# Second mixer of a fused three-layer kernel: the gated recurrence's work re-ordered on four engines' queues

## The chip, the core and the metric

One core of a Trainium2 chip runs the whole program. The time is that of the device, in microseconds (us), from three runs of the kernel before; a separate profiled execution gives the trace.

## The reference, cut to what matters

The program is two blocks in a row on 512 tokens of width 1024. The first block (two layers, each a mixer and a convolution FFN) is not touched. The second block's mixer is touched. It projects the normed input to 26 feature tiles of 128 (attention queries, keys, values; `hq`, `i`, `ff`, `fb`, `hg` for the recurrence), and the normed context of 256 tokens for 14 of them:

```python
def hgrn2_prep(q, i, f, lb_d):
    fg = lb_d + (1.0 - lb_d) * jax.nn.sigmoid(f)
    qh = sh(jax.nn.silu(q) * (HG_HEAD_DIM ** -0.5))
    return qh, sh(1.0 - fg), sh(i), sh(jnp.log(fg))
# S_t = diag(f_t) S_{t-1} + k_t v_t^T, o_t = S_t^T q_t, forward and backward, 4 heads,
# the state of the context is where the tokens start; then
# rmsnorm(o_f + flip(o_b), gain) * silu(g), beside softmax attention over 768 keys,
# both into @ w_out, and a SwiGLU FFN
```

## The kernel before, in words

Arrays lie with features on the 128 partitions and tokens on the free axis. A projection's weights come in chunks of 128x1024 (one output tile). For each chunk SP loads 512 KB, ACT makes the high part `w_hi` (line 160), DVE the low part `w_lo` (166), and PE runs three matmuls for each of 8 pieces of the depth (196).

**The slots.** In the mixer PE's work for chunks 2 to 25 is cut into 76 slots (`PARTS`). A chunk with a context half has four slots (two of 12 matmuls on 512 tokens, which I call x slots, then two of 12 on 256 context tokens, c slots). The others have two x slots. `SB_LIST` gives the order of the chunks, `FIRST` a chunk's first slot, `ENDED` the slot at which a chunk has ended. Each engine's program is written out by hand over these slots. What it does in slot p comes in a fixed order, and every engine executes its own queue in that order.

**The recurrence.** There are 4 heads, two directions each (u = 0 to 7), and 7 levels for each direction: 56 jobs, n = 7u + level. One job goes through DVE `difference` (2278, 2279), ACT exponential (`decays`, 2145), POOL's two products into `gla_mixed` (2043, 2044), PE `level` (2432, 8 matmuls) and DVE `select` (2301). The rings are short: `dec` has 4 buffers, so a difference waits for the product of job n - 4. `gla_mixed` has 3, so the product of job n waits for `level` n - 3. `level` waits for `select` n - 2.

**Around the jobs** lies work of each head or direction, placed with `due(n, first, every, number)`:
- ACT `sigmoid` of the gates (2081); from head 2 on it is preceded by the query's Silu (2076). POOL `gates` (2009), keys (2014, 2015) and their sum (2019). ACT `gate_logs` (2087), which waits for the keys. DVE `sum_gates` (four scans, 2265, 2267). All this has to be done for a head before its first difference.
- ACT `prepare` (2096 to 2100); POOL `to_end` (2024, 2025); PE `turn_values` and `turn_keys` (2442, 2449), all through PSUM bank 5; ACT `v_out` (2117) and `kd_out` (2109), which empty that bank one turn at a time; PE `sums` (2459, 2462); DVE `states`.
- PE `diagonal`, `output` and `mean`; ACT `diag_out`, `o_out` (2130, 2131) and `o_rstd` (2137 a logarithm, 2139 an exponential); DVE's scaling with it (2318).

Before, DVE, ACT and POOL are at job p - 11 in slot p (`AHEAD`) and PE at job p - 14 (`PE_AT`). `result(c)` on ACT empties a chunk's banks (2066 for the context, which bank 2 holds alone, 2069 for the tokens) and then makes `w_hi` of chunk c + 2. The first c slot of a chunk waits for the context copy of the chunk before. At slot 72 ACT runs `head_rstd` (2177, 2180), the attention's six rstd tiles. After the last slot come the splits of keys and queries (2221, 2202), the Silu of the four `hg` tiles (2225) and 32 units of attention (`logits` 2563, 2564; softmax 2238, 2385, 2390; transposes; values 2591).

ACT has function tables: where one instruction needs another set than the one before, the program holds an ACT_TABLE_LOAD. Silu, Sigmoid, Ln and Exp each have one of their own in the trace.

Of the kernel before, what the change touches and what calls it, by code (L numbers as in the profile page):

```python
# [78 lines left out]
def build(nc, A, out):  # L79
    with ExitStack() as ctx:  # L80
# [1682 lines left out]
        def layer(l, out_name, x_base=None, mods=None):  # L1763
# [18 lines left out]
        SB_LIST = [("hq", 0), ("hq", 1), ("ff", 0), ("fb", 0), ("i", 0), ("ff", 1), ("fb", 1), ("i", 1),  # L1782
                   ("hq", 2), ("ff", 2), ("fb", 2), ("i", 2), ("hq", 3), ("ff", 3), ("fb", 3), ("i", 3),
# [83 lines left out]
        ctx_out, hg_in, late_hi = sem("ctx_out"), sem("gate_in"), sem("late_hi")  # L1867
# [11 lines left out]
        AHEAD = 11  # L1879
        PE_AT = 14  # L1880
# [89 lines left out]
        class SecondMixer(Stage):  # L1970
# [26 lines left out]
            def gpsimd(self, pool):  # L1997
# [6 lines left out]
                def gates(hd):  # L2004
                    pool.wait_ge(g["sig"], 4 * hd + 5)
                    for d in range(2):
                        u, t = 2 * hd + d, d * HG + hd
                        for f in (bx(u), bc(u)):
                            nc.gpsimd.tensor_scalar(f, f, lbs[:, 5, t:t + 1], lbs[:, 0, t:t + 1], ALU.mult, ALU.add)\
                                .then_inc(g["fg"], 1)  # L2010
                    for d in range(2):
                        u = 2 * hd + d
                        pool.wait_ge(g["fg"], 2 * u + 2)
                        nc.gpsimd.tensor_scalar(kx[:, u % 4, :], bx(u), -1.0, 1.0, ALU.mult, ALU.add).then_inc(g["k"], 1)
                        nc.gpsimd.tensor_scalar(kc[u % 4][:, :], bc(u), -1.0, 1.0, ALU.mult, ALU.add).then_inc(g["k"], 1)
                    pool.wait_ge(g["k"], 4 * hd + 4)
# [18 lines left out]
                gates(0)  # L2035
                for n in range(JOBS):
# [19 lines left out]
            def scalar(self, act):  # L2056
# [5 lines left out]
                def result(c):  # L2062
# [4 lines left out]
                    if name == "hg":  # L2067
                        act.wait_ge(g["mult"], JOBS)
                    self.emptied(nc.scalar.activation(sb_hT[:, X_TILE[name](m), :], bank[c % 2][:, :],
                                                      ACT.Silu if c < SPLIT else ACT.Copy), c)  # L2070
                    self.high(act, 0, c, c + SPLIT < w.n)

                def sigmoid(hd):
                    if hd >= 2:
                        self.there(act, SB_LIST.index(("hq", hd)))
                        nc.scalar.activation(hq(hd), hq(hd), ACT.Silu)
# [64 lines left out]
                def decays(n):  # L2141
# [4 lines left out]
                    hd = due(n, 2, 2 * LEVELS, HG)  # L2146
# [36 lines left out]
                for p in range(len(PARTS)):  # L2183
                    if p in ENDED:
                        result(ENDED[p])
                    hd = due(p, 20, 14, HG - 1)
                    if p == 8 or hd is not None:
                        sigmoid(0 if p == 8 else hd + 1)
                    hd = due(p, 23, 14, HG - 1)
                    if p == 11 or hd is not None:  # L2190
                        gate_logs(0 if p == 11 else hd + 1)
                    decays(p - AHEAD)
# [4 lines left out]
                    if p == 72:  # L2197
                        head_rstd()
# [19 lines left out]
                act.wait_ge(b["scaled"], NT)  # L2218
                for kv in range(2):
# [3 lines left out]
                for m in range(HG):  # L2223
                    self.there(act, SB_LIST.index(("hg", m)))
                nc.scalar.activation(sb_hT[:, HG_TILE:HG_TILE + HG, :], sb_hT[:, HG_TILE:HG_TILE + HG, :], ACT.Silu).then_inc(hg_in, 1)
                for u in range(U2 + HIGH + 1):
                    if u < TAIL:
                        decays(len(PARTS) - AHEAD + u)
# [21 lines left out]
            def vector(self, dve):  # L2250
# [9 lines left out]
                def sum_gates(hd):  # L2260
                    dve.wait_ge(g["ln"], 4 * hd + 4)
                    dve.wait_ge(g["inside"], 2)
                    for u in (2 * hd, 2 * hd + 1):
                        turn = slice(None, None, 1 if u % 2 == 0 else -1)
                        nc.vector.tensor_tensor_scan(bx(u)[:, turn], inside[:, :], bx(u)[:, turn], 0.0, ALU.mult, ALU.add)\
                            .then_inc(g["scan"], 1)
                        nc.vector.tensor_tensor_scan(bc(u)[:, turn], bc(u)[:, turn], bc(u)[:, turn], 0.0, ALU.add, ALU.bypass)\
                            .then_inc(g["scan"], 1)
# [35 lines left out]
                def gla(n):  # L2304
                    hd = due(n, -1, 2 * LEVELS, HG)
# [4 lines left out]
                    u = due(n, 10, LEVELS, U7)  # L2310
# [4 lines left out]
                    hd = due(n, 26, 2 * LEVELS, HG)  # L2315
                    if hd is not None:
# [449 lines left out]
```

## Time and profile before

| what | us |
|---|---|
| three runs, lowest, median, highest | 2270.62, 2271.0, 2272.22 |
| the profiled execution | 2270.88 |
| its span | 2269.2 |
| PE busy | 2097.4 (92%) |
| DVE, ACT, POOL busy | 1239.7, 902.1, 317.0 |
| mean granted clock of PE | 0.962 |
| first recurrence level on PE, last | 1406.0, 1683.7 |

Times within the span count from its start. A busy share says how long an engine had an instruction running. A stall is time in which PE had none. The granted clock says at which of its two levels (1.2 and 2.4 GHz) PE ran: 1.00 is 2.4 GHz all the time.

### The profile page before, as it was taken

To read this page: it belongs to the slowest core of one execution; us is meant where nothing else is said; L and a number is where in the kernel's file an instruction comes from. 1 tells how busy PE (TensorE), PEld (TensorE's weight loads), DVE (VectorE), ACT (ScalarE), POOL (GpSimd) and SP (SyncE) were. 2 spreads that over 40 slices of the span, in tenths; PEclk is the share of its full clock that TensorE was granted. 3 is DMA by queue.
4 is the path that set the end of the run, shared out by engine and by line. 5 is a ranking of instruction groups with operands and counts; after the bars stand their busy time and mean duration, and the time that the engine had idled before them with its cause. 6 is when DMAs were issued, how large, how long until landed. Compare 5 with 4: busy or idle time off the path is not lost. (4 is left out here: it accounts for less than half of the span.)

```text
span 2269.2 us, 27321 instructions
## 1 busy us (share of the span) xinstructions
PE 2097.4 (92%) x9710; PEld 1660.5 (73%) x9710; DVE 1239.7 (55%) x1922; ACT 902.1 (40%) x1396; POOL 317.0 (14%) x404
## 2 busy tenths in 40 slices
PE   8999878999999899999999978878887898999997
PEld 6666547888888777778888847767765676888886
DVE  3666437788767656756564353555556534333333
ACT  4433533444422344344442244455447624223222
POOL 0033310101000211000000023455420002000000
PEclk9999899999999999999999989889898999999999
DMA  5211002556444322222333212100110022232321
GB/s 182 77 55 38 1 19 75 172 189 194 156 160 156 102 84 84 75 84 92 94 107 106 91 37 65 38 29 29 56 47 1 1 75 66 92 102 92 118 92 50
DMA packets 52628, 191.84 MB, mean 85 GB/s; under 512 B 5792, under 2 KB 8512, under 8 KB 52288
## 3 DMA queue, kind: packets, MB, share of 16 engines
q1 hardware_dynamic: 44672, 163.07, 22.3%
q0 software_dynamic: 7344, 27.27, 3.8%
q8 instruction: 50, 0.82, 0.1%
q10 hardware_dynamic: 528, 0.40, 0.1%
q14 instruction: 34, 0.28, 0.0%
HBM read 187.05 MB, written 3.67 MB: 84 GB/s over the span
## 5 line engine op out<-in xcount | busy, mean ns | idle before, releaser
L196 PE MATMUL psum<-xH,w_hi 128*128 128x512 f32 x1800 | 731.0, 406 | 42.8 <-DVE xL L1301 22.7
L196 PE MATMUL psum<-xL,w_hi 128*128 128x512 f32 x1800 | 713.1, 396 | 0.0
L196 PE MATMUL psum<-xH,w_lo 128*128 128x512 f32 x1800 | 712.7, 396 | 0.0
L166 DVE TENSOR_TENSOR w_lo<-w_raw,w_hi 128x1024 fp32r<-128x1024 f32 (+1 forms) x273 | 355.5, 1303 | 381.4 <-ACT w_hi L160 381.3
L160 ACT ACTIVATE w_hi<-w_raw 128x1024 fp32r<-128x1024 f32 (+1 forms) x273 | 303.1, 1111 | 399.7 <-PE psum L196 395.2
L196 PEld LDWEIGHTS psum<-xH,w_hi 128*128 128x128 f32 x1800 | 345.1, 192 | 144.2 <-DVE xL L1301 37.9
L196 PEld LDWEIGHTS psum<-xH,w_lo 128*128 128x128 f32 x1800 | 345.0, 192 | 74.5
L196 PEld LDWEIGHTS psum<-xL,w_hi 128*128 128x128 f32 x1800 | 345.5, 192 | 71.2 <-issue 3.1
L196 PE MATMUL psum<-hidH,w_hi 128*128 128x512 f32 x528 | 206.2, 391 | 0.0
L196 PE MATMUL psum<-hidH,w_lo 128*128 128x512 f32 x528 | 205.4, 389 | 0.0
L196 PE MATMUL psum<-hidL,w_hi 128*128 128x512 f32 x528 | 205.4, 389 | 0.0
L1376 DVE SCALAR_TENSOR_TENSOR gate_value<-psum,cols,gate_value 128x511 f32<-128x511 f32 x88 | 66.0, 750 | 132.2 <-ACT gate_value L1349 131.2
L1349 ACT ACTIVATE gate_value<-psum,cols 128x512 f32<-128x512 f32 x88 | 60.7, 689 | 162.6 <-PE psum L196 162.6
L1312 POOL TENSOR_SCALAR xT<-y,cols 128x512 f32<-128x512 f32 x32 | 39.4, 1240 | 555.6 <-DVE y L1293 555.6
L196 PEld LDWEIGHTS psum<-hidH,w_hi 128*128 128x128 f32 x528 | 99.1, 188 | 21.0 <-issue 0.5
L196 PEld LDWEIGHTS psum<-hidL,w_hi 128*128 128x128 f32 x528 | 99.1, 188 | 20.9 <-issue 0.5
L196 PEld LDWEIGHTS psum<-hidH,w_lo 128*128 128x128 f32 x528 | 99.1, 188 | 20.7
L2301 DVE COPY_PREDICATED gla_weights<-gla_masks,psum 128x512 f32<-128x512 uint8 x56 | 41.3, 738 | 76.9 <-PE psum L2432 75.2
L2145 ACT ACTIVATE sb_hT<-sb_hT 128x512 f32<-128x512 f32 x56 | 34.9, 629 | 112.4 <-DVE sb_hT L2279 112.3
L612 ACT ACTIVATE logits<-logits,stat 128x128 f32<-128x128 f32 (+3 forms) x64 | 36.0, 562 | 108.2 <-DVE stat L740 108.0
L740 DVE CUSTOM_DVE_ANT_0 logits<-psum,addend 128x128 f32<-128x128 f32 (+3 forms) x64 | 31.4, 490 | 83.7 <-PE psum L846 81.7
L2432 PE MATMUL psum<-gla_mixed 128*128 128x128 f32 x448 | 62.3, 284 | 13.8 <-POOL gla_mixed L2044 13.8
(314 smaller groups left out, 2546.4 us busy)
## 6 DMA issues: line engine op xcount, KB each, us to landing
w_raw<-in_up SPq DMA_DIRECT2D x132, 512.0 KB, 3.5
w_raw<-in_down SPq DMA_DIRECT2D x48, 704.0 KB, 4.0
mod_raw<-in_mod POOLq DMA_DIRECT2D x48, 512.0 KB, 3.9
w_raw<-in_sb_in SPq DMA_DIRECT2D x26, 512.0 KB, 3.5
w_raw<-in_ev_in SPq DMA_DIRECT2D x23, 512.0 KB, 3.6
w_raw<-in_od_in SPq DMA_DIRECT2D x20, 512.0 KB, 3.5
w_raw<-in_ev_out SPq DMA_DIRECT2D x8, 512.0 KB, 3.6
w_raw<-in_od_out SPq DMA_DIRECT2D x8, 512.0 KB, 3.5
```

Source lines behind the costliest of these rows:

```text
L160: nc.scalar.activation(w_hi[:, s % SPLIT, 0:w.cols], raw[:, s, 0:w.cols], ACT.Copy).then_inc(w.high, 1)
L166: nc.vector.tensor_tensor(w_lo[:, s % SPLIT, 0:w.cols], raw[:, s, 0:w.cols], w_hi[:, s % SPLIT, 0:w.cols].bitcast(F32), ALU.subtract).then ...
L196: mm = nc.tensor.matmul(acc, a[:, slot % SPLIT, cut], b[:, k0 + k, :], start=start and n == 0, stop=stop and n == 2)
L612: nc.scalar.activation(t, t, ACT.Exp, bias=stat[:, 0, s:s + 1], scale=-1.0, accum_out=stat[:, 1, s:s + 1]).then_inc(a["exp"], 1)
L740: nc.vector.tensor_tensor_reduce(out=tl[:, s % RING, 0:n], in0=logits_bank(s)[:, 0:n], in1=Xa[:, s % 3, 0:n], scale=-1.0 if kind == "a" el ...
L1312: nc.gpsimd.tensor_scalar(dst, yt[:, t % 3, 0:self.n], self.gain(t), self.shift(t), ALU.mult, ALU.add)\
L1349: nc.scalar.activation(value if j % 2 else gate, bank[j % 2][:, :], ACT.Copy, scale=self.tap(i, j, 2)).then_inc(ff["tap"], 1)
L1376: nc.vector.scalar_tensor_tensor(y[:, 1:T], acc[:, 0:T - 1], self.tap(i, j, 1), y[:, 1:T], ALU.mult, ALU.add).then_inc(ff["conv"], 1)
L2145: nc.scalar.activation(d, d, ACT.Exp).then_inc(g["exp"], 1)
L2301: nc.vector.copy_predicated(aT[:, hd % 2, :, :], level_mask[d][:, l * P:(l + 1) * P].unsqueeze(1).to_broadcast([P, NB, P]), bank[3 + n % 2 ...
L2432: mm = nc.tensor.matmul(bank[3 + n % 2][:, blk(c)], x[:, blk(c)], x[:, blk(c)], start=True, stop=True)
```

## The change

It touches the second mixer alone. The output, the matmuls and the loads stay the same. Chunks `hq2` and `hq3` come forward to places 4 and 5 of the order. ACT, DVE and POOL are at job p - 14 in slot p and PE at job p - 19. What was done per head in one go is spread over more slots.

```diff
-        SB_LIST = [("hq", 0), ("hq", 1), ("ff", 0), ("fb", 0), ("i", 0), ("ff", 1), ("fb", 1), ("i", 1),
-                   ("hq", 2), ("ff", 2), ("fb", 2), ("i", 2), ("hq", 3), ("ff", 3), ("fb", 3), ("i", 3),
+        SB_LIST = [("hq", 0), ("hq", 1), ("ff", 0), ("fb", 0), ("hq", 2), ("hq", 3), ("i", 0), ("ff", 1), ("fb", 1), ("i", 1),
+                   ("ff", 2), ("fb", 2), ("i", 2), ("ff", 3), ("fb", 3), ("i", 3),
...
-        AHEAD = 11
-        PE_AT = 14
+        AHEAD = 14
+        LEAD = LAG = 5
+        PE_AT = AHEAD + LEAD
+        SIGMOID = {8: 0, 24: 1, 36: 2, 48: 3}
+        LOGS = {11: 0, 27: 1, 39: 2, 53: 3}
...
+                gates_at = {c - AHEAD: hd for c, hd in SIGMOID.items() if hd}
...
-                    if l == 2:
+                    if l == 5:
                         to_end(u)
-                    hd = due(n, 9, 2 * LEVELS, HG - 1)
-                    if hd is not None:
-                        gates(hd + 1)
+                    for d in range(2):
+                        if n - d in gates_at:
+                            gates(gates_at[n - d], d)
+                    if n - 2 in gates_at:
+                        keys(gates_at[n - 2])
+                    if n - 3 in gates_at:
+                        key_sum(gates_at[n - 3])
...
-                        act.wait_ge(g["mult"], JOBS)
+                        act.wait_ge(g["mult"], JOBS - 4 + m + 1)
...
-                                                      ACT.Silu if c < SPLIT else ACT.Copy), c)
+                                                      ACT.Silu if name in ("hq", "hg") else ACT.Copy), c)
...
-                    if hd:
-                        act.wait_ge(g["y"], hd)
+                    act.wait_ge(*((g["y"], hd) if hd else (g["to_end"], 4)))
...
+                def around(n):
+                    hd = due(n, LEAD - 1, 2 * LEVELS, HG)
                     if hd is not None:
                         diag_out(hd)
-                    u = due(n, 1, LEVELS, U7)
+                    u = due(n, 4, LEVELS, U7)
                     if u is not None:
                         prepare(u)
                     for half in range(2):
-                        hd = due(n, 4 + half, 2 * LEVELS, HG)
+                        hd = due(n, LEAD + 2 * half, 2 * LEVELS, HG)
                         if hd is not None:
                             v_out(hd, half)
-                        u = due(n, 6 + half, LEVELS, U7)
+                        u = due(n, LEAD + 4 + 2 * half, LEVELS, U7)
                         if u is not None:
                             kd_out(u, half)
-                    hd = due(n, 22, 2 * LEVELS, HG)
+                    hd = due(n, LEAD + 18, 2 * LEVELS, HG)
                     if hd is not None:
                         o_out(hd)
-                    hd = due(n, 24, 2 * LEVELS, HG)
-                    if hd is not None:
+                    hd = due(n, LEAD + 20, 2 * LEVELS, HG)
+                    if hd not in (None, 2):
                         o_rstd(hd)
...
                 for p in range(len(PARTS)):
+                    decay(p - AHEAD)
                     if p in ENDED:
                         result(ENDED[p])
...
+                    if p in SIGMOID:
+                        sigmoid(SIGMOID[p])
+                    if p in LOGS:
+                        gate_logs(LOGS[p])
+                    around(p - AHEAD)
...
                     if p == 72:
+                        o_rstd(2)
                         head_rstd()
...
                 act.wait_ge(b["scaled"], NT)
+                act.wait_ge(g["kv"], U7)
...
-                for m in range(HG):
-                    self.there(act, SB_LIST.index(("hg", m)))
-                nc.scalar.activation(sb_hT[:, HG_TILE:HG_TILE + HG, :], sb_hT[:, HG_TILE:HG_TILE + HG, :], ACT.Silu).then_inc(hg_in, 1)
...
+                def jobs(n):
+                    hd = due(n, 0, 2 * LEVELS, HG)
                     if hd is not None:
-                        sum_gates(hd)
+                        sum_gates(2 * hd)
                     if 0 <= n < JOBS:
                         difference(n)
...
+                def around(n):
+                    hd = due(n, 3, 2 * LEVELS, HG)
+                    if hd is not None:
+                        sum_gates(2 * hd + 1)
+                    u = due(n, LEAD + 8, LEVELS, U7)
                     if u is not None:
                         states(u)
-                    if 3 <= n < JOBS + 3:
-                        select(n - 3)
...
+                    if LAG <= n < JOBS + LAG:
+                        select(n - LAG)
...
+                dve.wait_ge(g["kv"], U7)
+                for n in range(2):
+                    dve.wait_ge(b["v_turned"], n + 1)
...
                 def gla(n):
                     if 0 <= n < JOBS:
                         level(n)
...
+                    for half in range(2):
+                        hd = due(n, 2 * half - 1, 2 * LEVELS, HG)
+                        if hd is not None:
+                            turn_values(hd, half)
+                        u = due(n, 3 + 2 * half, LEVELS, U7)
+                        if u is not None:
+                            turn_keys(u, half)
+                    u = due(n, 7, LEVELS, U7)
+                    if u is not None:
+                        sums(u)
-                    hd = due(n, 18, 2 * LEVELS, HG)
+                    hd = due(n, 17, 2 * LEVELS, HG)
                     if hd is not None:
                         output(hd)
```

`sum_gates` takes one direction instead of a head, DVE's `jobs` comes before the low part of a chunk, and `o_rstd` of head 3 and its scaling now fall into units 5 and 7 of the attention.

## Rows read from the trace of the kernel before

**Rows 1.** The page: PE's busy time, share of the span, instructions.
```profile
PE 2097.4 (92%) x9710; PEld 1660.5 (73%) x9710; DVE 1239.7 (55%) x1922; ACT 902.1 (40%) x1396; POOL 317.0 (14%) x404
```
**Rows 2.** Busy time by stretch: PE, PEld, DVE, ACT, POOL, PE's granted clock, DMA.
```profile
1375.00:1693.70 318.70, 262.53 (x1577) 227.95 (x1575) 168.38 (x262) 152.24 (x262) 142.79 (x169) 0.92 0.12 37
1400.00:1421.00 21.00, 14.49 (x80) 12.27 (x80) 12.54 (x20) 10.73 (x21) 9.31 (x12) 0.84 0.16 49
1581.40:1606.00 24.60, 13.25 (x58) 10.96 (x57) 9.27 (x15) 9.03 (x15) 13.28 (x19) 0.65 0.08 22
1646.70:1693.70 47.00, 39.10 (x191) 29.79 (x189) 24.28 (x36) 15.81 (x26) 14.74 (x13) 1.00 0.08 23
```
**Rows 3.** Waits of PE between 1375 and 1840: us, times, longest.
```profile
PE psum L2449 <- ACT gla_kd_tm L2109: 23.8, 5, 7.2
```
**Rows 4.** Timeline of PE, levels of head 0: start, length (us).
```profile
1426.65 1.06 PE L2432 MATMUL psum<-gla_mixed 128*128 128x128 f32 x8
1428.98 1.06 PE L2432 MATMUL psum<-gla_mixed 128*128 128x128 f32 x8
1433.74 1.05 PE L2432 MATMUL psum<-gla_mixed 128*128 128x128 f32 x8
1437.37 1.05 PE L2432 MATMUL psum<-gla_mixed 128*128 128x128 f32 x8
```
**Rows 5.** Timeline of POOL, ACT and DVE, change from head 2 to head 3.
```profile
1576.89 0.74 POOL L2043 TENSOR_TENSOR gla_mixed<-sb_hT 128x256 f32<-128x256 f32 x1 [7.93 <-ACT sb_hT L2145]
...
1578.47 1.20 POOL L2024 TENSOR_TENSOR gla_keys_decayed<-gla_keys_decayed,gla_k 128x384 f32<-128x384 f32 x1
...
1580.35 1.20 POOL L2009 TENSOR_SCALAR sb_hT<-sb_hT,gla_lb 128x512 f32<-128x512 f32 x1
...
1583.90 0.62 POOL L2014 TENSOR_SCALAR gla_k<-sb_hT 128x512 f32<-128x512 f32 x1
...
1585.88 0.63 ACT L2087 ACTIVATE sb_hT<-sb_hT 128x512 f32<-128x512 f32 x1 [2.78 <-POOL gla_kc L2015]
...
1587.66 1.28 ACT L2145 ACT_TABLE_LOAD   x1
...
1591.32 1.28 DVE L166 TENSOR_TENSOR w_lo<-w_raw,w_hi 128x1024 fp32r<-128x1024 f32 x1 [8.57 <-ACT w_hi L160]
1592.52 1.21 DVE L2265 TENSOR_TENSOR_SCAN sb_hT<-gla_inside,sb_hT 128x512 f32<-128x512 f32 x1
...
1595.94 0.39 DVE L2278 TENSOR_TENSOR sb_hT<-sb_hT 128x256 f32<-128x256 f32 x1
...
1596.70 0.63 ACT L2145 ACTIVATE sb_hT<-sb_hT 128x512 f32<-128x512 f32 x1 [5.41 <-DVE sb_hT L2279]
```
**Rows 6.** Timeline of ACT at 1496.5: `prepare`, `o_out`, `result`, then a table load.
```profile
1496.53 0.62 ACT L2096 ACTIVATE gla_since<-sb_hT 128x512 f32<-128x512 f32 x1
...
1498.33 0.57 ACT L2130 ACTIVATE sb_hc<-psum 128x512 f32<-128x512 f32 x1
...
1499.28 0.37 ACT L2066 ACTIVATE sb_hc<-psum 128x256 f32<-128x256 f32 x1
...
1501.11 1.28 ACT L2076 ACT_TABLE_LOAD   x1
1502.40 0.63 ACT L2076 ACTIVATE sb_hT<-sb_hT 128x512 f32<-128x512 f32 x1
```
**Rows 7.** Timeline of ACT, end of the slots.
```profile
1695.00 1.28 ACT L2177 ACT_TABLE_LOAD   x1
...
1704.11 0.57 ACT L2069 ACTIVATE sb_hT<-psum 128x512 f32<-128x512 f32 x1
...
1710.13 1.70 ACT L2221 ACTIVATE keys_split<-keys 64x768 fp32r<-64x768 f32 x2
```
**Rows 8.** Timeline of PE, logits of unit 0 and of unit 7.
```profile
1713.68 0.55 PE L2563 MATMUL psum<-keys_split,queries_split 128*128 128x256 f32 x1 [3.21 <-DVE queries_split L2367]
...
1735.13 0.36 PE L2563 MATMUL psum<-keys_split,queries_split 128*128 128x256 f32 x1
```

More of the change, by code:

```diff
@@ L2002, in gpsimd, with gates, keys @@
                 pool.wait_ge(g["lb"], LB_STEPS)
-                def gates(hd):
+                def gates(hd, d):
                     pool.wait_ge(g["sig"], 4 * hd + 5)
[L2006 to L2010, printed above, removed]
+                    u, t = 2 * hd + d, d * HG + hd
+                    for f in (bx(u), bc(u)):
+                        nc.gpsimd.tensor_scalar(f, f, lbs[:, 5, t:t + 1], lbs[:, 0, t:t + 1], ALU.mult, ALU.add)\
+                            .then_inc(g["fg"], 1)
+                def keys(hd):
                     for d in range(2):
@@ L2033, in rotated @@
                         .then_inc(b["cos"], 1)
-                gates(0)
+                gates(0, 0)
+                gates(0, 1)
+                keys(0)
+                key_sum(0)
+                gates_at = {c - AHEAD: hd for c, hd in SIGMOID.items() if hd}
                 for n in range(JOBS):
@@ L2067, in result @@
                     if name == "hg":
-                        act.wait_ge(g["mult"], JOBS)
+                        act.wait_ge(g["mult"], JOBS - 4 + m + 1)
                     self.emptied(nc.scalar.activation(sb_hT[:, X_TILE[name](m), :], bank[c % 2][:, :],
-                                                      ACT.Silu if c < SPLIT else ACT.Copy), c)
+                                                      ACT.Silu if name in ("hq", "hg") else ACT.Copy), c)
                     self.high(act, 0, c, c + SPLIT < w.n)
                 def sigmoid(hd):
-                    if hd >= 2:
-                        self.there(act, SB_LIST.index(("hq", hd)))
-                        nc.scalar.activation(hq(hd), hq(hd), ACT.Silu)
+                    self.there(act, SB_LIST.index(("hq", hd)))
                     self.there(act, SB_LIST.index(("ff", hd)))
@@ L2222, in scalar @@
                     queries_high(0, kv)
[L2223 to L2225 removed]
                 for u in range(U2 + HIGH + 1):
                     if u < TAIL:
[L2228 removed]
+                        around(len(PARTS) - AHEAD + u)
                     if OUT <= u < U2 + OUT:
@@ L2258, in gain_of, with sum_gates @@
                     return cols[:, at_g:at_g + 1]
-                def sum_gates(hd):
-                    dve.wait_ge(g["ln"], 4 * hd + 4)
+                def sum_gates(u):
+                    dve.wait_ge(g["ln"], 2 * u + 2)
                     dve.wait_ge(g["inside"], 2)
[L2263 to L2268, printed above, removed]
+                    turn = slice(None, None, 1 if u % 2 == 0 else -1)
+                    nc.vector.tensor_tensor_scan(bx(u)[:, turn], inside[:, :], bx(u)[:, turn], 0.0, ALU.mult, ALU.add)\
+                        .then_inc(g["scan"], 1)
+                    nc.vector.tensor_tensor_scan(bc(u)[:, turn], bc(u)[:, turn], bc(u)[:, turn], 0.0, ALU.add, ALU.bypass)\
+                        .then_inc(g["scan"], 1)
                 def difference(n):
@@ L2338, in vector @@
                         self.low(dve, 0, 0, True)
+                    jobs(p - AHEAD)
                     if p in ENDED and ENDED[p] + SPLIT < w.n:
@@ L2343, in vector @@
                         nc.vector.tensor_copy(level_mask[p - 2][:, :], masks_in[p - 2][:, :])
-                    gla(p - AHEAD)
+                    around(p - AHEAD)
+                    if p == 73:
+                        normed(2)
                     if p in GAINS:
@@ L2378, in vector @@
                     if u < TAIL:
-                        gla(len(PARTS) - AHEAD + u)
+                        around(len(PARTS) - AHEAD + u)
                     if 0 <= v < U2:
@@ L2395, in vector @@
                     if hd is not None:
-                        dve.wait_ge(hg_in, 1)
+                        self.there(dve, SB_LIST.index(("hg", hd)))
                         dve.wait_ge(g["y"], hd + 1)
@@ L2493, in gla @@
                         level(n)
-                        u, l = n // LEVELS, n % LEVELS
-                        if l < 2 and u % 2 == 0:
-                            turn_values(u // 2, l)
-                        if l in (2, 3):
-                            turn_keys(u, l - 2)
-                        if l == 5:
-                            sums(u)
-                    hd = due(n, 18, 2 * LEVELS, HG)
+                    for half in range(2):
[9 more added lines that the diff above has]
+                    hd = due(n, 17, 2 * LEVELS, HG)
                     if hd is not None:
                         output(hd)
-                    hd = due(n, 20, 2 * LEVELS, HG)
+                    hd = due(n, 19, 2 * LEVELS, HG)
                     if hd is not None:
@@ L2552, in logits @@
                     else:
[L2553 removed]
+                        pe.wait_ge(b["v_out"], 1)
                         pe.wait_ge(g["pred"], JOBS)
```

47 lines of the change are left out of this document (18 added, 29 removed).

## The prediction

> **What bounds the kernel now.** I read the page first. PE is busy 92% of the span [rows 1], so only work taken off PE, or stalls and slow clock taken away, can shorten the run. This change takes nothing off PE. So I asked how much PE stands still in the second mixer. Up to 1693.7, where slot 72 begins, the busy time by stretch gives 318.7 - 262.5 = 56.2 us of stall, and a granted clock of 0.92: 2 x 0.08 x 318.7 = 51 us at 1.2 GHz instead of 2.4 [rows 2]. Some 28 of these 51 are stall (the three long waits below and a little before each). In the other 23 the work took twice its time, so the clock cost 11.7. Together 67.9 us stand to be had before slot 72. They lie in four places. The start, 1400 to 1421: 21.0 - 14.5 = 6.5 of stall, clock 0.84 [rows 2]. Three changes of head, alike: 24.6 - 13.25 = 11.35 in the one shown, clock 0.65 [rows 2]. Slots 62 to 71: 47.0 - 39.1 = 7.9 [rows 2]. Short waits between: the rest, 56.2 - 6.5 - 34.0 - 7.9 = 7.8. The waits say what ends a change of head: five waits of PE for `kd_out`, 23.8 us, the longest 7.2 [rows 3]. The timeline of the other engines shows the chain behind it: POOL's product, `to_end`, gates, keys, then ACT's logarithms (ACT had waited 2.78 for them), ACT's high part, DVE's low part, four scans, difference, exponential [rows 5]. ACT and DVE take their queues in order, so copies that PE needs stand behind this chain.
>
> **Durations.** From one level to the next PE takes 2.33 in a c slot and 3.63 in an x slot; a level is 1.05, or 0.85 of PE's time in sequence [rows 4]. The product of a job takes 1.58 (1576.89 to 1578.47), `to_end` 1.88, gates 3.55, keys 1.98, four logarithms 1.78, the low part 1.20, two scans 1.71 (half of 1592.52 to 1595.94), a difference 0.76 [rows 5]. `prepare` takes 1.80, `o_out` 0.95, `result` with a context copy 1.83, a table load 1.28 with 0.63 for the function behind it [rows 6]. Other copies on ACT are taken at 0.4 to 0.6, as those.
>
> **Part by part.** *The start.* Job 0's product was late for PE's slot 14. Now ACT, DVE and POOL begin it three slots later and PE five. The three chunks ahead of it have two slots less of context, and the Silu of `hq2` and `hq3` adds two loads (2.6) to ACT, which waits for PE at each chunk anyway. Gone through queue by queue with the durations above, an estimate: the first product is there near 1409, and PE comes to it near 1416. The cover is 7 us; I cost the start at 0 (was 6.5 and some 2.1 of clock).
>
> *The change to head 1.* The gates' pieces hang on jobs 10 to 13, and `mixed` has three buffers: the product of job 12 waits for level 9, in PE's slot 28. ACT's logarithms stand in slot 27, so ACT stands still until PE is past slot 28. From the start of level 9: 1.2 to the product, 1.6 product, 1.9 `to_end`, 2.0 keys, 0.9 two logarithms, 1.7 scans, 0.8 difference, 0.6 exponential, 0.4 context copy: 11.1. PE needs that copy for slot 30, at 5.0. Next late is DVE's low part, and behind it the select for level 11: 14.4 against 6.4. Cost 8.0, and 1.2 of clock.
>
> *To head 2.* Keys again wait, for level 21 in slot 40. ACT in slot 39 has the logarithms, `prepare(3)` and `kd_out(2, 1)`, which PE's `sums(2)` needs right after level 21. Chain: 1.2 + 1.6 + 2.0 + 1.8 + 1.3 (load for the exponential) + 1.8 + 0.4 = 10.1, against 0.9. The grouping with `o_rstd(0)` gives nothing, since `prepare(3)` stands between: two more loads and 1.3 us of functions, one exponential, `result` 1.8, low part 1.2, select 0.7, and level 23 comes at 18.2 against 7.1. Cost 11.1, clock 0.6 (its own wait covers the rest).
>
> *To head 3.* Sigmoid stands 8 slots ahead. Only `sums(4)` in slot 54 waits, 10.1 against 7.3: 2.8, and 1.0 of clock. The three changes: 9.2 + 11.7 + 3.8 = 24.7, where they cost 34.0 and 9.6.
>
> *New short waits.* `to_end(u)` now comes after level 5's product, which waits for PE's slot 7u + 21, and `turn_keys` wants it in slot 7u + 22: 4.7 after that level's start against 3.2 where a c slot lies between (slots 22, 43, 50: 1.5 each) and 4.5 elsewhere (0.2): 5.3 in all. `turn_values` of heads 1 to 3 (slots 32, 46, 60) wants `kd_out` of ACT's same slot, behind `prepare` and `diag_out`: 3.1, 1.4 and 3.1, by the same addition. In slots 62 to 71 the attention's means wait for DVE's select and rotation as before: 0.6 + 1.4 + 1.0 + 2.1 = 5.1 (was 7.9, of which the moved `o_rstd(2)` was 2.1). The last is larger than before, as Silu's load now stands in `result(22)`, ahead of DVE's low part. Sum before slot 72: 24.7 + 5.3 + 7.6 + 5.1 = 42.7, against 67.9.
>
> *From slot 72 on.* Three levels, a sum and a transpose move behind the mark: -4.4 before it. ACT empties chunk 23 and, 0.1 before the mark, starts `o_rstd(2)` (3.9) and `head_rstd` (1704.11 - 1695.00 = 9.1 [rows 7]), then a load, Silu and `kd_out(7, 1)`: +15.2. PE, ready at +14.5, does `sums(7)` to 16.6. Now both engines wait for it, DVE copies values and scales (4.3), and the splits begin at +20.9; they began at 1710.13, +16.4 [rows 7]. First logits 3.55 later [rows 7, 8], at +24.5; they were at +20.0. Then I save the Silu of `hg` (1.9 and a load) and `o_rstd(3)` in front of the second exponential, and pay `states(7)`, `output(3)` at half clock, `mean(3)` and `o_rstd(3)` (3.8) in units 0 to 5. Worked through unit by unit, unit 7's logits come at +48.3; they were at +41.4 (1735.13 [rows 8]). +6.9, of which 4.4 is the moved work. Beyond unit 7 nothing differs. The weights' loads keep their number; two go four to eight places earlier on SP's queue, which has had the buffers free each time, and no wait is added on it.
>
> **Sum.** 42.7 - 67.9 - 4.4 + 6.9 = -22.7. The profiled execution took 2270.9 (span 2269.2, 1.7 around it) and stands 0.1 under the median 2271.0: 2248.2, and 2248.3 against the median. I say 2248.
>
> What the trace does not show is how low the clock falls after the new stalls. From below it costs nothing after them; from above all work for 6 us after each of three, as in the stretch at 0.65 [rows 2], 3 x 3 = 9. I took 2.8, nearer the low end, since new waits cover part of it.
>
> **Rivals.** *A, the leads cover the changes of head.* If POOL runs so far ahead that keys and logarithms are done before ACT is wanted, the three changes cost nothing: 2248 - 25 = 2223. For it speaks the distance of 5 jobs; against it the ring of three, which pins POOL to three jobs ahead of PE. *B, the waits only move.* The chain behind a level is as long as before, so each change costs what it did, 14.5 with its clock: 43.6 instead of 24.7, giving 2267, within 0.2% of no change (a measurement of this kernel can tell about that much). For it: POOL still follows PE, and 11 us of chain is no shorter. Against it: at head 3 five slots lie between. *C, slower: both chains at each change.* If the copy for the context (8.0) and `kd_out` (11.1) are late one after the other at all three, with 3 of clock, each costs 22: 66 instead of 24.7, giving 2290. It decides once a change costs over 17 on average. Against it: by the slots the two are late together only at head 2.
>
> *D, the tables.* If a change of table held ACT 1.4 longer than the load, as long again, head 2 would cost 4 more and the end, with its five changes, 7 more: 2248 + 11 = 2259. If a logarithm and an exponential needed only one load between them, the grouping would be idle and the end 5 shorter: 2243. Against both: the function starts 0.01 behind its load [rows 6], and `head_rstd` begins with a load for its logarithms [rows 7] though exponentials ran before it. Both lie inside the forecast's own range, chance together 0.01, counted with it.
> The Trainium skill (ScalarE: Activation LUTs, What ACT_TABLE_LOAD costs) states the first: 1283 ns of load and some 1380 ns of drain for each switch; this trace shows the load and no drain.
> The same page (Table sets) states the second, one load for a logarithm followed by an exponential; this trace doesn't agree.
>
> That the order isn't what it says can't be, as each queue is written out.
>
> **Chances.** Forecast 0.70, A 0.12, B 0.09, C 0.09. Faster by over 0.2% (4.5 us): forecast and A, 0.82. Same: B, 0.09. Slower: C, 0.09. The forecast's own range: the small waits and clock together can be off by some 18 either way, 2230 to 2267. Reaching to B's side makes it 2230 to 2268. It leaves out A and C, 0.21.
>
> **What would show it.** Right: no stall between slots 12 and 22; waits of PE for a context copy near 6 us at slot 30, for `kd_out(2, 1)` near 9 at slot 40, under 4 at slot 54; many waits for `to_end` of about 1.5; ACT waiting for the keys at two changes; a load between the logarithms of slot 39 and `o_rstd(0)`; a gap of some 8 us before the first logits. Wrong: no wait of PE over 3 us at slots 28 to 42 (A); a stall of 11 at head 3 too (B, C); a first logit earlier than 23 after slot 72, or units 5 to 7 with no gap.

## The result, and the profile after

| | median us | runs | ratio to the kernel before, 95% interval |
|---|---|---|---|
| before | 2271.6 | 4 | |
| after | 2286.2 | 4 | 1.0064 [1.0049, 1.0079] |

The change is 14.6 us slower; the forecast was 2248, 23 us faster, with a range to 2268. Of the four places in which the prediction saw 67.9 us to be had, the start gave its share and the changes of head gave a part. Slots 62 to 71, which it had left nearly alone, took more than that back.

The page gives the busy time of each engine. PE does the same number of instructions as in [rows 1]:

```profile
PE 2100.3 (92%) x9710; PEld 1664.0 (73%) x9710; DVE 1240.8 (54%) x1922; ACT 899.8 (39%) x1394; POOL 321.5 (14%) x404
```

Busy time by stretch, with the columns of [rows 2]: the mixer up to slot 72, its start, the changes to head 1 and to head 2, and slots 61 to 71:

```profile
1375.00:1700.40 325.40, 263.88 (x1529) 229.23 (x1528) 162.05 (x250) 148.15 (x256) 143.24 (x166) 0.92 0.12 36
1404.50:1425.50 21.00, 21.00 (x137) 19.03 (x137) 15.04 (x26) 11.29 (x22) 10.03 (x12) 1.00 0.21 71
1446.00:1480.20 34.20, 22.76 (x124) 20.04 (x123) 17.07 (x24) 13.76 (x26) 17.04 (x21) 0.84 0.10 31
1500.00:1555.00 55.00, 37.40 (x226) 33.60 (x225) 28.80 (x42) 24.38 (x43) 26.10 (x31) 0.84 0.06 20
1618.90:1700.40 81.50, 63.11 (x300) 49.12 (x299) 31.17 (x53) 24.59 (x43) 24.14 (x28) 0.90 0.08 26
```

Slot 72 begins at 1700.4, where it began at 1693.7. The start is full, 21.00 busy of 21.00, at a granted clock of 1.00. Slot 61 begins at 1619.0, before the change at 1633.3: 14.3 us had been won by there. Slots 61 to 71 then take 81.5 us where they took 60.4 (1633.3 to 1693.7), with 18.4 us of stall and a clock of 0.90.

The waits of PE up to slot 72 (line waited on, releaser; total, times, longest), where [rows 3] had five long ones for `kd_out`:

```profile
PE psum L2480 <- ACT gla_kd_tm L2121: 14.4, 3, 8.8
PE psum L2463 <- ACT gla_kd_tm L2121: 12.5, 3, 5.4
PE psum L2549 <- ACT sb_hT L2185: 8.1, 2, 7.6
PE psum L196 <- ACT sb_hc L2080: 7.5, 1, 7.5
PE psum L2470 <- POOL gla_keys_decayed L2031: 5.9, 5, 1.9
PE psum L2549 <- ACT gla_k L2185: 5.5, 1, 5.5
PE psum L2544 <- DVE head_sin L2348: 4.8, 3, 2.0
...
```

With the two groups below them (2.2 and 0.5) they add up to 61.5 us (56.2 before). L2480 is `sums` and L2463 `turn_values`. L2549 is `head_turn`, PE's turn of an attention tile for its rotary embedding, and L2544 the mean of such a tile. L196 with L2080 is the context copy, L2470 `turn_keys`. The two waits of 7.6 and 5.5 at `head_turn` were in no step of the prediction. The timelines of POOL, DVE, ACT and PE around the first of them (start, length, instruction; in brackets the idle time ahead of it and what ended it) show where it is from:

```profile
1659.71 0.73 POOL L2053 TENSOR_TENSOR gla_mixed<-sb_hT 128x256 f32<-128x256 f32 x1 [5.92 <-PE psum L2453]
...
1661.08 1.26 POOL L2038 TENSOR_TENSOR head_rot<-sb_hT,rope 128x512 f32<-128x512 f32 x1
1653.99 0.68 DVE L2348 TENSOR_TENSOR head_sin<-psum,rope 128x512 f32<-128x512 f32 x1
1662.45 0.69 DVE L2352 TENSOR_TENSOR sb_hT<-head_rot,head_sin 128x512 f32<-128x512 f32 x1 [7.77 <-POOL head_rot L2038]
1663.85 0.63 ACT L2156 ACTIVATE sb_hT<-sb_hT 128x512 f32<-128x512 f32 x1 [12.06 <-DVE sb_hT L2289]
...
1666.44 0.58 ACT L2185 ACTIVATE sb_hT<-psum 128x512 f32<-128x512 f32 x1
1658.51 1.05 PE L2453 MATMUL psum<-gla_mixed 128*128 128x128 f32 x8
1667.16 2.05 PE L2549 MATMUL psum<-sb_hT,rope_turn 128*128 128x512 f32 x2 [7.60 <-ACT sb_hT L2185]
```

A tile's rotation has two halves: POOL multiplies by the cosines (`rotated`, L2038), DVE by the sines (L2348), and DVE adds them (L2352). POOL's half for turn v stands behind job n = c - 13, c being the slot in which DVE scales that tile (`GAINS`). The line reads `n + AHEAD - 1 in GAINS` in both kernels, but `AHEAD` went from 11 to 14: before, it was job c - 10. With three buffers job n's product waits for level n - 3. PE now does that level in slot n + 16 = c + 3; before, it did it in slot n + 11 = c + 1. DVE wants the rotation in slot c + 2 (c + 3 for the first turn). In the kernel before it lay ready, here for the same turn in POOL's and DVE's timelines:

```profile
1663.44 2.25 POOL L2032 TENSOR_TENSOR head_rot<-sb_hT,rope 128x512 f32<-128x512 f32 x1
1667.95 0.69 DVE L2334 TENSOR_TENSOR sb_hT<-head_rot,head_sin 128x512 f32<-128x512 f32 x1
```

After the change DVE has its half done at 1654.67 and then stands 7.8 us. Its differences behind that are late, and ACT's decay waits 12.1 for them. Behind the decay stand `prepare`, `kd_out` and the copy of the attention head's mean, and PE waits for that copy. By this theory 13 us of stall (7.60 + 5.54), and the low clock that follows each, come from rotations that are late; the runs below test it.

### The profile page after: what moved, and what is told of

Same layout as the page of the kernel before. It is cut to its first block and busy times, and to the rows that moved or that the text cites. A ratio compares the mean times of both kernels' runs of the same rounds, so it can differ in the third digit from the quotient of the medians.

```text
span 2283.4 us, 27323 instructions
## 1 busy us (share of the span) xinstructions
PE 2100.3 (92%) x9710; PEld 1664.0 (73%) x9710; DVE 1240.8 (54%) x1922; ACT 899.8 (39%) x1394; POOL 321.5 (14%) x404
## 5 line engine op out<-in xcount | busy, mean ns | idle before, releaser
L196 PE MATMUL psum<-xH,w_hi 128*128 128x512 f32 x1800 | 730.9, 406 | 43.2 <-DVE xL L1301 23.0
L196 PE MATMUL psum<-xL,w_hi 128*128 128x512 f32 x1800 | 712.1, 396 | 0.0
L196 PE MATMUL psum<-xH,w_lo 128*128 128x512 f32 x1800 | 711.8, 395 | 0.0
L196 PEld LDWEIGHTS psum<-xH,w_hi 128*128 128x128 f32 x1800 | 344.8, 192 | 145.9 <-DVE xL L1301 39.0
L196 PEld LDWEIGHTS psum<-xH,w_lo 128*128 128x128 f32 x1800 | 344.5, 191 | 74.4
L196 PEld LDWEIGHTS psum<-xL,w_hi 128*128 128x128 f32 x1800 | 345.3, 192 | 71.5 <-issue 3.7
L196 PE MATMUL psum<-hidH,w_hi 128*128 128x512 f32 x528 | 206.2, 391 | 0.0
L196 PE MATMUL psum<-hidH,w_lo 128*128 128x512 f32 x528 | 205.4, 389 | 0.0
L196 PE MATMUL psum<-hidL,w_hi 128*128 128x512 f32 x528 | 205.4, 389 | 0.0
L196 PEld LDWEIGHTS psum<-hidL,w_hi 128*128 128x128 f32 x528 | 99.1, 188 | 21.1 <-issue 0.5
L196 PEld LDWEIGHTS psum<-hidH,w_hi 128*128 128x128 f32 x528 | 99.1, 188 | 21.1 <-issue 0.5
L196 PEld LDWEIGHTS psum<-hidH,w_lo 128*128 128x128 f32 x528 | 99.1, 188 | 20.4
L2156 ACT ACTIVATE sb_hT<-sb_hT 128x512 f32<-128x512 f32 x56 | 35.0, 629 | 135.6 <-DVE sb_hT L2289 135.6
L1379 DVE SCALAR_TENSOR_TENSOR gate_value<-psum,cols,gate_value 128x510 f32<-128x510 f32 x88 | 65.9, 749 | 11.1 <-DVE gate_value L1376 2.8
L2053 POOL TENSOR_TENSOR gla_mixed<-sb_hT 128x256 f32<-128x256 f32 x56 | 47.3, 845 | 165.4 <-PE psum L2453 152.6
```

Source lines behind the costliest of these rows:

```text
L196: mm = nc.tensor.matmul(acc, a[:, slot % SPLIT, cut], b[:, k0 + k, :], start=start and n == 0, stop=stop and n == 2)
L1379: self.emptied(nc.vector.scalar_tensor_tensor(y[:, 2:T], acc[:, 0:T - 2], self.tap(i, j, 0), y[:, 2:T], ALU.mult, ALU.add), j)
L2053: nc.gpsimd.tensor_tensor(mq, halves(hq(u // 2), u, l)[0], eq, ALU.mult)
L2156: nc.scalar.activation(d, d, ACT.Exp).then_inc(g["exp"], 1)
```

## The experiments

Each edit is made to the kernel after the change, or to the run that is named. Gains are taken against the change's 2286.2, or against the run named:

| run | edit | median us | ratio to before, 95% interval |
|---|---|---|---|
| e1_rotation | rotation two jobs earlier | 2274.4 | 1.0010 [1.0000, 1.0019] |
| e2_pieces | gate work two jobs earlier | 2275.5 | 1.0015 [1.0006, 1.0024] |
| e3_both | both | 2263.9 | 0.9964 [0.9951, 0.9978] |
| e4_turns | e3, `to_end` behind level 4, copies first | 2241.0 | 0.9862 [0.9847, 0.9877] |
| e5_toend | e3, `to_end` only | 2257.0 | 0.9937 [0.9924, 0.9951] |
| e6_copies | e3, copies only | 2247.6 | 0.9892 [0.9874, 0.9910] |
| e7_scale | e4, queries scaled before the wait | 2242.7 | 0.9874 [0.9859, 0.9889] |
| e8_block | e4, gate work in one block | 2243.1 | 0.9877 [0.9862, 0.9892] |
| e9_silu | e4, `hg` Silu as before | 2242.1 | 0.9859 [0.9844, 0.9874] |
| e10_order | e4, chunk order as before | 2246.7 | 0.9884 [0.9869, 0.9899] |
| e11_late | e4, rotation as in the change | 2257.7 | 0.9941 [0.9927, 0.9955] |
| e12_best | e7 and e9 together | 2240.4 | 0.9857 [0.9841, 0.9874] |

**The rotation (e1).**

```diff
-                    if n + AHEAD - 1 in GAINS:
-                        rotated(GAINS[n + AHEAD - 1])
+                    if n + 15 in GAINS:
+                        rotated(GAINS[n + 15])
...
-                    if [c for c, m in GAINS.items() if m == v][0] > JOBS + AHEAD - 2:
+                    if [c for c, m in GAINS.items() if m == v][0] > JOBS + 15 - 1:
```

> One expression of the change is completed: GpSimd writes the rotation's product of turn v behind the job two earlier, so that it waits for the level of slot p + 1, as in the kernel before, and not p + 3. Theory R (the rotation stands behind a level that TensorE does two slots later than it used to, VectorE waits for the rotation in slot p + 2, and through VectorE's differences ScalarE's copies of the head means come late): the 7.60 and 5.54 us that TensorE waits at the two turns L2549 fall to under 1 each, the two 6.8 us stretches at 1.2 GHz that follow them go with them, slots 61 to 71 take some 64 us instead of 81.5, and the time falls by 17 us to about 2269. Rival S (ScalarE is late by itself there, from its squares, means and the decays of head 3): the two waits stay over 4 us each with another releaser in front, and the time stays at 2284 to 2288.

Measured: 11.8 us faster than the change, where 17 were expected. DVE no longer waits for POOL, in DVE's and PE's timelines:

```profile
1656.33 0.69 DVE L2352 TENSOR_TENSOR sb_hT<-head_rot,head_sin 128x512 f32<-128x512 f32 x1
1661.05 1.10 PE L2549 MATMUL psum<-sb_hT,rope_turn 128*128 128x512 f32 x2
```

Both waits are gone; only the first `head_turn` still waits, 0.96 (0.51 in the change). From the last `turn_values` to the first logits it is 91.0 us (1619.8 to 1710.8) against 107.1 (1618.6 to 1725.7). That is 16.1 less, of which 11.4 are stall (18.4 to 7.0) and the rest the two stretches at 1.2 GHz. The theory holds, rival S falls. Some 2 of the 16.1 come back at the attention's first units, where the stretch at 1.2 GHz is 13.7 us long and not 6.8. Another 1.2 are lost ahead of slot 61 in this execution, as the mixer was that much later by there.

**The gate work (e2, e3).**

```diff
-                gates_at = {c - AHEAD: hd for c, hd in SIGMOID.items() if hd}
+                gates_at = {c - AHEAD - 2: hd for c, hd in SIGMOID.items() if hd}
```

> GpSimd's four pieces of gate work (gates, gates, keys, key sum) go two jobs earlier in its order, nothing else. Theory P (at a change of head ScalarE's logarithms stand behind keys that stand behind a level that TensorE does only some slots later, so that the three engines wait in a ring and the lead is used up): the 18.6 us that ScalarE waits for the keys (L2099 behind L2019) fall to under 5, the waits at the changes to head 1 and 2 (7.9 and 10.4 us) fall to a third, and with the clock that they cost the time falls by 10 to 20 us, to about 2271. Rival Q (the chain of ScalarE's sigmoid, two table loads and logarithms, and VectorE's sums, sets the change of head by itself): ScalarE's wait for the keys goes and the waits of TensorE stay within 2 us of what they were; 2283 to 2287.

> The edits of the two runs before it together. They touch different slots (the pieces slots 25 to 50, the rotation 61 to 71), so by both theories the gains add: about 2286 - 17 - 15 = 2254. If the pieces only move the wait to slots 61 to 71, or the rotation's wait only hides one behind it, the sum is less than half of that: 2270 or more.

Measured: e2 is 10.7 faster than the change, within what was expected, and e3 22.3. Since 11.8 + 10.7 = 22.5, the two add. e3 missed its 2254 by 10 because each had given some 5 less than the sum took. ACT's wait for the keys, after the change and in e2:

```profile
ACT sb_hT L2099 <- POOL gla_kc L2019: 18.6, 3, 10.5
```

```profile
ACT sb_hT L2099 <- POOL gla_kc L2019: 4.6, 3, 2.2
```

In the change ACT, at its logarithms for head 1 and 2, waits for keys that POOL issues behind a product held by a level of PE (10.5 and 6.6 us). With the keys two jobs earlier, the waits of PE at those changes of head are 1.3 + 1.5 and 3.0 + 1.7, where they were 7.5 + 0.5 and 8.8 + 1.6. Theory P holds. The distance of five slots to PE was worth nothing to work that is queued behind a product waiting for PE.

**The copies and `to_end` (e4, e5, e6).**

```diff
-                    if l == 5:
+                    if l == 4:
                         to_end(u)
...
                 def around(n):
-                    hd = due(n, LEAD - 1, 2 * LEVELS, HG)
-                    if hd is not None:
-                        diag_out(hd)
-                    u = due(n, 4, LEVELS, U7)
-                    if u is not None:
-                        prepare(u)
                     for half in range(2):
...
+                    hd = due(n, LEAD - 1, 2 * LEVELS, HG)
+                    if hd is not None:
+                        diag_out(hd)
+                    u = due(n, 4, LEVELS, U7)
+                    if u is not None:
+                        prepare(u)
```

> The two edits together, and the work at the end of a unit moved up: GpSimd's keys times the decay to the end one job earlier (behind level 4 in place of 5), and ScalarE's copies of the turned values and keys ahead of its diagonal and its exponentials in the same slot. If the short waits of TensorE at turned keys, sums and turned values (5.9 us at L2470, 12.5 us at L2463, 14.4 at L2480, together 32.8) come from this order, they fall by 10 us or more against the run before it, and the time with them: about 2244. If they come from the engines being late as a whole, the time is within 3 us of the run before it.

> The fourth run had two edits over the third (2263.9 to 2241.0). Here only the first stands: GpSimd's keys times the decay to the end behind level 4 in place of 5. Theory T (those keys come one slot late for TensorE's turn of them): the waits at L2470 (5.8 us) go and the waits at L2480 behind ScalarE's copy stay at some 9 us; with the clock 2252 to 2258. If the copies' place in ScalarE's slot was all of it: within 3 us of 2264.

> The other edit alone over the third run: ScalarE copies the turned values and keys ahead of the diagonal's copy and the four exponentials (0.6 + 1.5 us and the waits before them) that stood in front of them in the same slot. Theory C (TensorE's 13.2 us at L2463 and 9.2 at L2480 are waits for that order): they fall by 10 us or more, and with the stretches at 1.2 GHz behind them the time is 2248 to 2254. By theory T of the run before this one, those waits stay where the turned keys were late, and the time is 2258 or more. If each edit gives less than a third of the 23 us, they only work together.

Measured: `to_end` alone gives 6.8 (2263.9 to 2257.0), the copies alone 16.2 (to 2247.6), both 22.9: again they add. e5 is as expected, e4 and e6 are 3.0 and 0.4 better. ACT at the last copy of head 1's keys, after the change:

```profile
1549.23 0.63 ACT L2156 ACTIVATE sb_hT<-sb_hT 128x512 f32<-128x512 f32 x1 [3.59 <-DVE sb_hT L2289]
1549.77 0.58 ACT L2135 ACTIVATE gla_weights<-psum 128x512 f32<-128x512 f32 x1
...
1551.64 0.50 ACT L2112 ACTIVATE gla_keys_decayed<-sb_hc 128x256 f32<-128x256 f32 x1
1552.04 0.36 ACT L2121 ACTIVATE gla_kd_tm<-psum 128x256 f32<-128x256 f32 x1
```

and in e6:

```profile
1534.93 0.63 ACT L2156 ACTIVATE sb_hT<-sb_hT 128x512 f32<-128x512 f32 x1 [2.85 <-DVE sb_hT L2289]
1535.46 0.37 ACT L2121 ACTIVATE gla_kd_tm<-psum 128x256 f32<-128x256 f32 x1
```

In the change the copy starts 2.8 us behind the decay (L2156), because a diagonal and five exponentials stand between them; PE waits 5.4 for the copy. In e6 it is next, and PE waits 0.8. PE's waits at `turn_values` fall from 13.2 in e3 to 2.2 in e6, at `sums` from 8.3 to 0.3. Those at `turn_keys` rise from 5.8 to 11.3, as PE now comes sooner to keys that `to_end` has not finished; in e4 `to_end` is earlier, and they are gone. The waits of PE in e4, up to slot 72:

```profile
PE psum L196 <- ACT sb_hc L2080: 6.2, 3, 3.0
PE psum L2544 <- DVE head_sin L2348: 6.0, 3, 2.1
PE psum L2453 <- DVE gla_weights L2311: 5.8, 4, 2.3
PE psum L2463 <- ACT gla_kd_tm L2121: 5.1, 3, 3.6
...
```

With the three below (1.2, 1.1 and 0.5) it is 25.9 us in place of 61.5, and 20.4 us at 1.2 GHz in place of 54.4. With four edits of position, and the same number of instructions on every engine as the change, e4 is 1.4% faster than the kernel before.

**The rotation again (e11).** The first edit undone in e4.

> Over the fourth run (2241.0): the rotation goes back behind the later level, as the change has it. Alone it was worth 2286.2 - 2274.4 = 11.8 us. If it is a cost of slots 61 to 71 by itself, it is worth the same here: 2253 (the two waits of 7.6 and 5.5 us before L2549 are back). If the changes of head fed it, it is worth under 6: below 2247.

Measured: 16.7 slower than e4, more than the 11.8 expected. The waits are back:

```profile
1636.02 2.04 PE L2549 MATMUL psum<-sb_hT,rope_turn 128*128 128x512 f32 x2 [7.59 <-ACT sb_hT L2185]
1656.52 2.04 PE L2549 MATMUL psum<-sb_hT,rope_turn 128*128 128x512 f32 x2 [7.16 <-ACT gla_k L2185]
```

So it is a cost of slots 61 to 71 by itself. The second wait is 1.6 longer here than in the change; why was not taken apart.

**Parts of the change that the forecast had at little (e8, e9, e10).** In e8 the four pieces are one block behind job n - 1 of `gates_at`; in e9 `result` copies `hg` and one Silu over the four tiles stands ahead of the attention's units; in e10 `SB_LIST` is that of the kernel before.

> Over the fourth run (2241.0): GpSimd's gate work in one block of nine instructions (about 7.5 us) between two jobs, at the place of the second piece, in place of four pieces. Theory L (TensorE five slots behind has room for it: the chain of jobs slips by 7.5 us once a head, a lead of five slots of some 3.6 us takes it, and ScalarE's logarithms lose their 2.2 us wait for the keys): 2238 to 2244, so that the four pieces were worth nothing. Rival M (the lead is used up at a change of head as it is, with 2.3 + 2.1 us of waits there): the block adds 3 to 5 us a head, 2250 to 2256.

> Over the fourth run (2241.0): the Silu of the four hg tiles goes back from the banks' exit to one instruction over all four at the start of the attention, as before the change. Theory V (in the page's rows ScalarE has a Silu table load in two of its results in the last slots, and now needs one load and 1.9 us of function ahead of the first exponential, where TensorE waits for it): the first units of the attention come 2 to 3.5 us later, 2243 to 2245. If ScalarE has idle time there (7.0 and 3.6 us ahead of copies in the last slots, 2.9 ahead of the first exponential), no change within 1.5 us.

> Over the fourth run (2241.0): only the order of the weights' chunks goes back to that of the kernel before (hq2 and hq3 in places 8 and 12, not 4 and 5). Theory W (nothing before slot 36 needs hq2, and the first forget gates come two chunks sooner for head 1, the values for head 0 too): no change within 1.5 us. Rival X (the context chunks now lie under changes of head, and the copies at ScalarE that TensorE waits for, 6.2 us at L2080, fall on the logarithms): 3 us or more slower.

Measured: e8 is 2.1 us over e4, with the intervals of the ratios overlapping, so in time the four pieces are worth nothing that shows. The traces are less plain. Up to slot 72 PE's stall is 30.5 us in e8 against 26.0 in e4, and the time at 1.2 GHz is 10.2 against 20.4. The block costs some 4.5 of stall, and the clock gave about that back; whether it would do so with other edits is open.

e9 is 1.1 over e4, also nothing that shows. From the first logits to the transposes at L2600 (L2603 in e9) it is 25.8 us against 23.9, but PE's stall there is 9.5 in both. The difference is clock (0.70 against 0.79), and ACT's 3.2 us more of work lie in time in which it had stood idle. From the last head mean to the first logits it is 29.4 against 32.2, with 7.8 of stall against 8.8 and again the rest clock. So theory V's cost was not there, and the rival answer, idle time on ACT, holds.

e10 is 5.7 over e4, and the intervals just overlap. Its trace has 29.9 us of waits up to slot 72 against 25.9. At the change to head 1 `turn_values` waits 3.5 where it waited 0.15. At the change to head 2 the level waits 6.1 for DVE's select. In e4 it waits 1.5 there, but PE has stood 3.0 for a context copy just ahead, so the difference is 1.6. DVE's timeline at that place, in e10 and in e4:

```profile
1512.70 1.22 DVE L166 TENSOR_TENSOR w_lo<-w_raw,w_hi 128x1024 fp32r<-128x1024 f32 x1 [12.37 <-ACT w_hi L160]
...
1507.08 1.22 DVE L166 TENSOR_TENSOR w_lo<-w_raw,w_hi 128x1024 fp32r<-128x1024 f32 x1 [11.27 <-ACT w_hi L160]
```

and ACT's in e10:

```profile
1507.37 1.28 ACT L2150 ACT_TABLE_LOAD   x1
...
1509.83 1.28 ACT L2083 ACT_TABLE_LOAD   x1
1511.13 0.60 ACT L2083 ACTIVATE sb_hT<-psum 128x512 f32<-128x512 f32 x1
1511.62 1.05 ACT L160 ACTIVATE w_hi<-w_raw 128x1024 fp32r<-128x1024 f32 x1
```

`hq3`, emptied at the change to head 2 in the old order, brings its Silu and a load of 1.3 us (L2083) behind `o_rstd(0)`, ahead of the high part, and DVE's low part waits 1.1 us longer than in e4. That accounts for the smaller part of the 4 us of waits (elsewhere e10 waits 1 us less). The larger one, at `turn_values`, was not followed back. It is neither W nor X as put: waits for the context copy (L2080) are less in e10, 1.1 against 6.2.

**The end (e7, e12).** In e7 DVE scales tiles 2 to 5 before `dve.wait_ge(g["kv"], U7)`, tiles 0 and 1 behind it.

> Over the fourth run (2241.0): VectorE scales the four query tiles (4 x 0.64 us) ahead of its new wait for the last sums of keys and values, not behind it, where it had stood still for 4.4 us. Theory K (the chain of sums, VectorE's six scalings, ScalarE's splits sets the first logits): TensorE's 7.83 us before them fall by 2.0 to 2.6, and the time with it to 2238.5. If the scalings are held by ScalarE's square roots instead, or the clock takes it back, no change within 1 us.

> The fourth run with the two edits at its end together: VectorE scales the query tiles ahead of its wait for the last sums (2.4 us less before the first logits, by the trace of that run) and the Silu of the hg tiles stands at the start of the attention (by the trace of that run 1.4 us less from the last head mean to the values). If both lie on the path that sets the end: 2241.0 - 3.8, some 2237. If the start of the attention is set by something both leave alone: 2240 to 2243, as each alone gave.

Measured: PE's wait for the first logits falls from 7.8 us by the 2.4 expected:

```profile
1681.35 0.55 PE L2593 MATMUL psum<-keys_split,queries_split 128*128 128x256 f32 x1 [5.43 <-DVE queries_split L2393]
```

but the time does not: 2242.7. The profiled run has 20.4 us at 1.2 GHz between 1450 and 1540 where e4 has 13.6, at places that the edit does not touch. The 2.4 are also within what the runs of one kernel differ by (2239.0 to 2242.4 for e4), so what the edit is worth stays open. e12 gives 2240.4, as its second answer said, and is not to be told from e4. Both e4 and e12 are faster than the change by 2% and than the kernel before by 1.4%.

## Why the prediction was wrong, step by step

The working added stalls to the time that PE needs without any. Its steps, beside what the trace of the kernel after shows:

| step | predicted us | measured us |
|---|---|---|
| start | 0 | 0 |
| change to head 1 (context copy, select) | 8.0 | 7.5 + 0.5 |
| `sums(0)` for `kd_out` | not seen | 1.7 |
| change to head 2 | 11.1 | 8.8 + 1.6 |
| change to head 3 | 2.8 | 3.9 + 0.7 |
| `to_end`, five waits | 5.3 | 5.9 |
| `turn_values` | 7.6 | 12.5 |
| slots 62 to 71 | 5.1 | 18.4 |
| together | 39.9 | 61.5 |
| first logits behind slot 72 | 24.5 | 25.3 |
| unit 7's logits behind slot 72 | 48.3 | 48.0 |

**The step that failed** is "In slots 62 to 71 the attention's means wait for DVE's select and rotation as before". DVE's rotation was not as before: POOL's half of it moved behind a level two slots later, by a constant in its condition that the change raised. I had traced each queue at the changes of head and left the tail of POOL's queue unread. It cost 11.8 us alone (e1) and 16.7 with the other edits in (e11). The two waits at `head_turn` are 13.1 of the 18.4 us of stall there; the other 5.3 are what the prediction had (5.1). The step accounts for most of the 14.6 by which the change lost, but not for the 23 that were forecast: with the rotation put right (e1, 2274.4) the change still gains nothing. The rest is the clock and `turn_values`.

**The clock was mis-sized.** The prediction added 2.8 us of low clock to the new stalls and took 11.7 away. The sums of the busy times over the stretches at 1.2 GHz between 1375 and slot 72, before and after:

```profile
sum 51.30, PE 23.68 PEld 19.52 DVE 23.91 ACT 20.78 POOL 23.05; mean PE 5.92 PEld 4.88 DVE 5.98 ACT 5.20 POOL 5.76
```

```profile
sum 54.40, PE 40.80 PEld 34.38 DVE 16.77 ACT 30.43 POOL 2.42; mean PE 4.53 PEld 3.82 DVE 1.86 ACT 3.38 POOL 0.27
```

The time at low clock is nearly the same, 51.3 and 54.4 us. But before, PE stood still for over half of it, in four stretches; after, in nine, it worked for 40.8. An instruction takes twice as long there (L2549 2.05 us, against 1.02 at 2.4 GHz), so half of PE's busy time is lost: 11.8 before, 20.4 after. The prediction had only 2.8 for it. The upper bound named, 9, was too low as well: it counted three stalls, and nine stretches came. Eight stand behind single waits of 3.5 to 8.8 us, one behind two short waits close together (1.6 and 1.9).

**`turn_values`** was seen with the right mechanism (`kd_out` of the same slot behind `prepare` and `diag_out`) and the wrong size: 7.6 for 12.5. The addition began at the decay, and by the timeline at 1549 that had itself waited 3.6 us for DVE's difference. e6 shows the price of the copies' place, at `turn_values` and `sums` together and with its clock, to be 16.2 us.

The terms together: 21.6 of stall and 17.6 of clock more than predicted are 39.2; slot 72 came 36.3 later than predicted (1664.1). The 2.9 between are PE's work up to the mark, which was that much shorter than the one taken from the kernel before; no run shows why. **Right** were the start, the rings at head 1 and 2, the five short waits and everything behind slot 72. Rival B, that the waits only move, was the nearest in kind: the stall up to slot 72 was no less than before (61.5 and 56.2), though it moved to slots 61 to 71 and did not stay at the changes of head, and its 2267 was too low as well. C, the slower one, gave 2290, close to the 2286 measured, but that is luck: at no change of head do both chains cost 22. Rival D's two rules would have shown in the loads. This trace has again a load between logarithms and exponentials, with the function 0.01 behind it:

```profile
1514.96 0.40 ACT L2099 ACTIVATE sb_hc<-sb_hc 128x256 f32<-128x256 f32 x1
1515.38 1.28 ACT L2108 ACT_TABLE_LOAD   x1
1516.67 0.63 ACT L2108 ACTIVATE gla_since<-sb_hT 128x512 f32<-128x512 f32 x1
```

The Trainium skill (ScalarE: Activation LUTs, What ACT_TABLE_LOAD costs) adds some 1380 ns of drain to each load for another set; neither the trace before nor this one shows it.

## What to carry to other kernels

A larger lead (how many slots an engine works ahead of PE) moves every item whose place is written as a distance from it. List all of them, on every queue. For each, name the step of the bounding engine that the item ahead of it in the queue waits for, before and after. Some queues hold both products that must wait for PE, because a ring of buffers is short, and work that other engines want. That work belongs ahead of the waiting product. A copy that PE waits for belongs first in its slot, ahead of exponentials that are wanted later. Four such moves turned 0.6% slower into 1.4% faster.

## What was not expected of the hardware

In this kernel many short stalls cost more clock than few long ones. After the change one wait of 3.5 us (up to 1476.9) was enough for a stretch at 1.2 GHz, and PE then worked through most of it, 6.18 us busy of 6.80 (busy time by stretch):

```profile
1476.30:1483.10 6.80, 6.18 (x18) 5.06 (x19) 1.05 (x3) 1.71 (x4) 0.00 (x0) 0.52 0.25 80
```

Before, a stretch of 13.7 us at a change of head came behind a wait of 4.1 us and held one of 7.2, so a good part of it was lost anyway:

```profile
1450.20:1463.90 13.70, 6.16 (x19) 5.12 (x20) 6.63 (x10) 5.00 (x9) 5.34 (x7) 0.50 0.10 39
```

From the change to e4, 35.6 us of stall up to slot 72 went and 45.2 us of time.

Behind waits of some 2 us the clock is not to be foretold from these traces. The same wait at the last head mean, 1.95 us in e4 and 1.94 in e9, brought a stretch at 1.2 GHz in e4 (granted clock 0.50 from 1650.4 to 1653.8) and none in e9 (1.00 from 1646 to 1660). Differences of 1 or 2 us between such runs, and the gain of an edit that is no larger, can be this alone.
